# Transform tables brought as high and low parts by GpSimd's converting transfers, in a two-block sequence model on one core

## The reference, cut to what matters

```
def _hyena(hy, spec, skip):
    ...
    for o, gate in enumerate((g1, g2)):
        conv = jnp.fft.irfft(jnp.fft.rfft(z, n=2 * L, axis=1) * spec[:, o], n=2 * L, axis=1)[:, :L]
        z = gate * (conv + z * skip[o].astype(jnp.float32))
    return z
```

## Time and profile before

| what | value |
|---|---|
| median of 3 runs | 1792.31 us (1791.78 to 1796.0) |
| the profiled execution | 1793.52 us |
| its span, first to last instruction | 1791.7 us |
| mean granted TensorE clock | 0.982 |
| PE busy | 1716.9 us, 96% |
| DVE, ACT, POOL busy | 884.3, 665.2, 824.4 us |
| transferred | 167.55 MB, mean 94 GB/s |

### The profile page before, as it was taken

The page is one execution under the profiler, slowest core; times in us unless marked ns, Lnnn a source line. Parts: engine busy times, 40 slices in busy tenths (PEclk is TensorE's granted clock), DMA queues, the critical chain, the costliest instruction groups (busy, mean ns, idle before and its releaser), DMA issues.

```text
span 1791.7 us, 21383 instructions
## 1 busy us (share of the span) xinstructions
PE 1716.9 (96%) x7488; PEld 1379.8 (77%) x7488; DVE 884.3 (49%) x1172; ACT 665.2 (37%) x850; POOL 824.4 (46%) x610
## 2 busy tenths in 40 slices
PE   6899998889999999999999999999999999999996
PEld 4577776767876888888888788888888888888885
DVE  6658667774524452423256676763333432132235
ACT  4354443434422311112234657574333432222222
POOL 4225322666441454444444656555444354444443
PEclk9999999889999999999999999999999999999998
DMA  5112111224220222222222333332222232222222
GB/s 201 56 51 83 59 48 47 83 94 154 106 83 24 95 95 100 97 95 94 94 94 94 110 104 115 106 115 96 94 94 97 92 104 96 94 94 102 98 94 94
DMA packets 47343, 167.55 MB, mean 94 GB/s; under 512 B 5109, under 2 KB 5237, under 8 KB 47034
## 3 DMA queue, kind: packets, MB, share of 16 engines
q1 hardware_dynamic: 45728, 162.71, 26.1%
q10 hardware_dynamic: 1562, 4.13, 0.6%
HBM read 164.71 MB, written 2.10 MB: 93 GB/s over the span
## 4 chain that ended last, share of the span: by engine, by line
PE 43%; issue 21%; POOL 14%; DVE 2%; POOLq 0%; ACT 0%; DMA 0%; DVEq 0%; SPq 0%
POOL m_w_lo L486 14%; PE ps L525 14%; PE ps L526 14%; PE ps L527 14%; DVE m_TM L1868 0%; DVE m_h L2175 0%; DVE m_qs L1784 0%; DVE m_s L1467 0%; DVE m_ZL L1794 0%; DMA m_raw<-in_strips 0%; DVE m_s L1864 0%; POOL m_QL L504 0%; POOLq L494 0%; DVE m_QL L1856 0%; POOLq L492 0%
## 5 line engine op out<-in xcount | busy, mean ns | idle before, releaser
L486 POOL TENSOR_TENSOR m_w_lo<-m_raw,m_w_hi 128x512 fp32r<-128x512 f32 x600 | 810.1, 1373 | 930.8 <-ACT m_w_hi L1021 930.6
L1021 ACT ACTIVATE m_w_hi<-m_raw 128x1024 fp32r<-128x1024 f32 x300 | 316.6, 1057 | 627.1 <-DMA m_raw<-in_strips 626.8
L525 PE MATMUL ps<-m_XH,m_w_hi 128*128 128x512 f32 x1096 | 439.9, 401 | 4.8 <-POOL m_w_lo L486 4.5
L527 PE MATMUL ps<-m_XH,m_w_lo 128*128 128x512 f32 x1096 | 429.2, 392 | 0.0
L526 PE MATMUL ps<-m_XL,m_w_hi 128*128 128x512 f32 x1000 | 391.9, 392 | 0.0
L525 PEld LDWEIGHTS ps<-m_XH,m_w_hi 128*128 128x128 f32 x1096 | 207.5, 189 | 58.7 <-issue 9.5
L527 PEld LDWEIGHTS ps<-m_XH,m_w_lo 128*128 128x128 f32 x1096 | 207.3, 189 | 44.0
L526 PEld LDWEIGHTS ps<-m_XL,m_w_hi 128*128 128x128 f32 x1000 | 189.6, 190 | 40.5 <-issue 2.0
L525 PE MATMUL ps<-m_FH,m_w_hi 128*128 128x512 f32 x432 | 168.2, 389 | 0.3 <-DVE m_FL L1460 0.3
L526 PE MATMUL ps<-m_FL,m_w_hi 128*128 128x512 f32 x432 | 168.1, 389 | 0.0
L527 PE MATMUL ps<-m_FH,m_w_lo 128*128 128x512 f32 x432 | 168.1, 389 | 0.0
(11 more groups left out here) (344 smaller groups left out, 2243.1 us busy)
## 6 DMA issues: line engine op xcount, KB each, us to landing
m_raw<-in_strips SPq DMA_DIRECT2D x300, 512.0 KB, 3.2
m_x_in<-in_x SPq DMA_DIRECT2D x4, 512.0 KB, 11.6
m_x_res<-in_x ACTq DMA_DIRECT2D x1, 2048.0 KB, 8.5
out<-m_h SPq DMA_DIRECT2D x8, 256.0 KB, 2.1
m_decay<-in_decay ACTq DMA_DIRECT2D x1, 1024.0 KB, 10.2
m_memf<-in_mem SPq DMA_DIRECT2D x1, 1024.0 KB, 16.5
m_w<-in_w ACTq DMA_DIRECT2D x1, 512.0 KB, 8.0
m_const<-in_const ACTq DMA_DIRECT2D x1, 256.0 KB, 6.8
```

Source lines behind the costliest of these rows:

```text
L486: nc.gpsimd.tensor_tensor(w_lo[:, c], raw[:, c], f(w_hi[:, c]), ALU.subtract).then_inc(lo_ready, 1)
L525: pe.matmul(dst, w_hi[:, c], xh, start=first, stop=False)
L527: return pe.matmul(dst, w_lo[:, c], xh, start=False, stop=last)
L1021: act.activation(w_hi[:, c], raw[:, c], ACT.Copy).then_inc(hi_ready, 1)
```

## The change

The eleven table strips are split before the launch. The array of strips keeps their values rounded to the coarse format, and a new array `tables` holds the differences. For a table SP issues nothing, ScalarE computes nothing and only passes the signal on, and GpSimd issues two transfers, one into `w_hi` and one into `w_lo`. Their destination type is float32r and their source type float32, so they convert. Both signal the one semaphore `tab_in`. GpSimd waits for both before it signals `lo_ready`, ahead of everything that follows in its program. Strips up to 55 are written out one by one on SP and GpSimd, where there had been a loop.

```diff
+TABLES = tuple(range(S_SPEC, S_SPEC + N_SPEC)) + HY_STRIPS[0] + HY_STRIPS[1]
...
+            for n in range(RING, S_WOUT):
+                sp.wait_ge(pe_done, n - RING + 1)
+                if n not in TABLES:
+                    load(n, n % RING)
...
             def lows(first, end):
 
-                full, rest = divmod(end - first, RING)
-                if full:
+                for n in range(first, min(end, S_WOUT)):
+                    if n in TABLES:
+                        c = slice(n % RING * STRIP, (n % RING + 1) * STRIP)
+                        pool.wait_ge(pe_done, n - RING + 1)
+                        pool.dma_start(w_hi[:, c], A["strips"][n]).then_inc(tab_in, 16)
+                        pool.dma_start(w_lo[:, c], A["tables"][TABLES.index(n)]).then_inc(tab_in, 16)
+                    pool.wait_ge(hi_ready, n + 1)
+                    if n in TABLES:
+                        pool.wait_ge(tab_in, 32 * (TABLES.index(n) + 1))
+                        pool.wait_ge(lo_ready, 2 * n)
+                        pool.sem_inc(lo_ready, 2)
+                    else:
+                        low(n % RING)
...
-                act.wait_ge(landed[slot], count * 16)
                 c = slice(slot * STRIP, (slot + 1) * STRIP)
-                act.activation(w_hi[:, c], raw[:, c], ACT.Copy).then_inc(hi_ready, 1)
+                if n in TABLES:
+                    act.wait_ge(hi_ready, n)
+                    act.sem_inc(hi_ready, 1)
+                else:
+                    act.wait_ge(landed[slot], count * 16)
+                    act.activation(w_hi[:, c], raw[:, c], ACT.Copy).then_inc(hi_ready, 1)
...
+    tables = all_strips[list(TABLES)]
+    coarse = ((tables.view(np.uint32) + np.uint32(0x800)) & np.uint32(0xFFFFF000)).view(np.float32)
+    all_strips[list(TABLES)] = coarse
```

More of the change, by code:

```diff
@@ L299, in build @@
         hi_ready = sem("hi_ready")
+        tab_in = sem("tab_in")
         lo_ready = sem("lo_ready")
@@ L446, in load @@
             def load(n, slot):
-                sp.dma_start(raw[:, slot * STRIP:(slot + 1) * STRIP], A["strips"][n]).then_inc(landed[slot], 16)
+                c = slice(slot * STRIP, (slot + 1) * STRIP)
+                sp.dma_start(raw[:, c], A["strips"][n]).then_inc(landed[slot], 16)
             def x_pair(i):
@@ L462, in _ @@
             sp.dma_start(memf[:], A["mem"]).then_inc(ld_mem, 16)
-            full, rest = divmod(N_STRIPS - RING, RING)
+            for n in range(RING, S_WOUT):
+                sp.wait_ge(pe_done, n - RING + 1)
+                if n not in TABLES:
+                    load(n, n % RING)
+            full, rest = divmod(N_STRIPS - S_WOUT, RING)
             with sp.Fori(0, full) as i:
                 for u in range(RING):
-                    sp.wait_ge(pe_done, i * RING + u + 1)
+                    sp.wait_ge(pe_done, i * RING + (S_WOUT - RING + u + 1))
                     sp.dma_start(raw[:, u * STRIP:(u + 1) * STRIP],
-                                 A["strips"][bass.ds(i * RING + (RING + u), 1)].rearrange("a p c -> (a p) c")
+                                 A["strips"][bass.ds(i * RING + (S_WOUT + u), 1)].rearrange("a p c -> (a p) c")
                                  ).then_inc(landed[u], 16)
             for u in range(rest):
-                n = RING + full * RING + u
+                n = S_WOUT + full * RING + u
                 sp.wait_ge(pe_done, n - RING + 1)
@@ L488, in lows @@
             def lows(first, end):
-                full, rest = divmod(end - first, RING)
-                if full:
+                for n in range(first, min(end, S_WOUT)):
[11 more added lines that the diff above has]
+                        low(n % RING)
+                if end > S_WOUT:
+                    full, rest = divmod(end - S_WOUT, RING)
                     with pool.Fori(0, full) as i:
                         for u in range(RING):
[L494 to L498, removed]
+                            pool.wait_ge(hi_ready, i * RING + (S_WOUT + u + 1))
+                            low((S_WOUT + u) % RING)
+                    for n in range(end - rest, end):
+                        pool.wait_ge(hi_ready, n + 1)
+                        low(n % RING)
             def product_low(o, j):
@@ L1017, in high, with loads @@
             def high(n, slot, count):
-                act.wait_ge(landed[slot], count * 16)
                 c = slice(slot * STRIP, (slot + 1) * STRIP)
-                act.activation(w_hi[:, c], raw[:, c], ACT.Copy).then_inc(hi_ready, 1)
+                if n in TABLES:
[4 more added lines that the diff above has]
+                    act.activation(w_hi[:, c], raw[:, c], ACT.Copy).then_inc(hi_ready, 1)
+            def loads(n):
+                return n // RING + 1 - sum(t < n and t % RING == n % RING for t in TABLES)
             def ahead(n):
@@ L1026, in ahead @@
                 if m < N_STRIPS:
-                    high(m, m % RING, m // RING + 1)
+                    high(m, m % RING, loads(m))
             def ahead_in(turn, per, n):
                 m = n + 3
-                high(None, m % RING, turn * (per // RING) + (m // RING + 1))
+                high(None, m % RING, turn * (per // RING) + loads(m))
             def root(n, dst=rstd):
@@ L2315 @@
     arrays = {
-        "strips": all_strips, "const": const, "feat": features, "w3": w3,
+        "strips": all_strips, "tables": tables - coarse, "const": const, "feat": features, "w3": w3,
         "decay": decay.reshape(TT, P, T).transpose(1, 0, 2).reshape(P, TT * T),
```

## The result

The changed kernel takes 1798.88 us (median of 20 runs, 1793.47 to 1803.8), the kernel before 1792.37 us (20 runs, 1784.46 to 1797.05). The ratio is 1.0036, 95% interval [1.0023, 1.005]: slower, by 6.5 us. Measured again later it was 1799.79 against 1791.99 us, ratio 1.0046 [1.0028, 1.0063]. The forecast was 1800.7, range 1788 to 1823.

The account below looks back on a forecast made before the run. The prediction took PE as the bound, busy 1716.9 of 1791.7 us. Late values in the Hyena stage (+9.2 us) and the filter's spectrum (-0.8) gave +8.4 on 1792.3, so 1800.7 us, range 1788 to 1823.

Parts of the forecast that it names:

- The mechanism: Hyena stage: GpSimd idles about 7 us per table, seven times; PE waits 6 us and 10 us for its QL.
- X: Time from GpSimd being free to issue a table's first transfer until both halves are complete; taken as 7.0 us.
- The bound of 5.0 us for the pair: Lower bound for landing a table's two 512 KB transfers, from SP's loads: 3.2 + 1.8 us.
- The rule: Whole kernel's change in us: 7X - 40.6 above X = 5.7, 4X - 23.5 below; break-even at X = 5.8.
- the rule's tail: Hyena stage, from the end of QL(1,0) to the values: 13.8 us of work plus 0.3 for handovers, 14.1 us.
- The sign of being wrong: End of the Hyena stage: values beginning before 412 us, instead of near 419, would point to A.
- ScalarE's relief: Roundings of about 1.06 us removed from ScalarE; claimed to reach PE in one place only, -0.8 us.
- Ahead of the filter's spectrum: Rounding of strip 10 precedes the squares of `mem`, whose sum holds PE 0.82 us; removing it gives -0.8 us.
- Costed at nothing: Tables 8 to 10, table 32, the 11 extra halves (5.6 MB), SP's skipped loads and written-out loops: no cost.
- A: Rival: table transfers as quick as SP's, X = 5.0 to 6.5, change -3.5 to +4.9 us; chance 0.34.
- B: Rival: VectorE holds up GpSimd's transfer descriptors, X = 9.6, change +26.6 us, 1819 us; chance 0.12.
- C: Rival: converting halves the transfer rate, X = 10.6, change +33.6 us, 1826 us; chance 0.08.

Follow-up runs that it names:

- e1: Changed kernel, but TensorE instead of GpSimd waits for each table to land, one semaphore per slot: 1782.32 us, ratio 0.9955 against the kernel before.
- e3: Kernel before with only tables 44 to 47 handled the new way: 1795.85 us, ratio 1.0036 against the kernel before.
- e4: Kernel before with only tables 8, 9, 10 and 32 handled the new way: 1790.86 us, ratio 1.0001 against the kernel before.
- e5: Changed kernel, but GpSimd issues a table's second transfer only when its first has landed: 1813.22 us, ratio 1.0125 against the kernel before.
- e6: Changed kernel with only the first 128 of 1024 columns of each table half transferred: 1785.53 us, ratio 0.9965 against the kernel before.
- e2: Kernel before with only tables 37, 38 and 39 handled the new way: 1796.11 us, ratio 1.003 against the kernel before.
- e7: Kernel before without GpSimd's low parts of the eleven tables; TensorE's third matmul reads the high part instead: 1783.41 us, ratio 0.9947.
- e8: e1 with the 2 MB transfer of x issued some 20 us later, behind strip 54's rounding: 1785.55 us, ratio 0.9959 against the kernel before.
- e9: The changed kernel run once more, unaltered, for a second profile: 1799.79 us, ratio 1.0046 against the kernel before.

## Why the prediction was right, and where its numbers were off

**The mechanism** held: GpSimd waits inside its program, the products behind the tables come late, and PE waits for them. PE's two largest waits are those named, 7.3 us at inverse(0,1) (6 forecast) and 6.3 at inverse(1,0) (10 forecast); in the second profile 5.7 and 10.0. e1, e3 and e4 show it by taking it away and by placing it, e5 and e6 by making X longer and shorter. A table kept GpSimd for 5.1 to 7.4 us, where about 7 were forecast.

**X was mis-sized**: 7.0 forecast, 6.0 and 6.3 measured, 6.15 in the mean. At 7 us per us this term made the forecast 6 us too high. The bound of 5.0 us for the pair was met where nothing else was in transit: both halves of table 37 had landed 5.0 us after the first issue, of table 45 4.9 to 5.0. That includes the two issues (0.53 to 0.57 us each), so the 1.2 us for them were counted twice, and of the 0.8 us for VectorE (the rows that it names give 0.95) nothing is to be seen. What was left out is the meeting with SP's loads: X is 5.3 in the mean for tables 37 and 45, and 6.3 (5.1 to 7.4) for 38, 39, 46 and 47, beside which a strip is loaded. That is read from traces, no run took these loads away. Table 44, with no strip beside it, took 6.8 and 7.3; why is open.

**The rule** for the stage nearly held. With the stage's start at 315.4 it reads 54.5 + 7X above the kink and 71.6 + 4X below it, in us to the values:

| | X | rule | measured |
|---|---|---|---|
| e6 | 3.5 | 85.6 | 84.0 |
| changed, first profile | 6.0 | 96.5 | 98.4 |
| changed, second profile | 6.3 | 98.6 | 100.2 |
| e5 | 8.2 | 111.9 | 113.5 |

Three of the four are 1.6 to 1.9 us above the rule. e6's nearness is in part chance: its first inverse ended 43.4 us after the stage's start, where the rule below the kink keeps the first profile's 47.6.

**What made up for X.** By the rule alone X = 6.15 gives 97.6 - 94.2 - 0.8 = +2.5 us, and 6.5 to 7.8 were measured. Three terms make up the difference.

First, the kernel before was read in a slow execution of its stage: 94.2 us, against 90.6 in its second profile and 90.2 in e4. Of the 3.6 us between its profiles 2.4 are inverse(0,3), which took 5.3 us in the first (363.04 - 357.78) and 2.8 in the second and in e4, behind the same wait of 2.7 us: the lower clock that the prediction read from the earlier trace rows does not follow that wait each time. Behind the changed kernel's longer wait it did: inverse(0,1) to (0,3) took 10.9 us, the 5.3 + 2.8 + 2.8 of the forecast. Against the mean of both, the rule gives 1.8 us more.

Second, the rule's tail is too short: from the end of QL(1,0) to the values it has 14.1 us, and the changed kernel, e5 and e6 take 15.7. GpSimd's low of strip 48 and its two QLs take 8.1 for 7.4, and VectorE's product of step 3 ends 2.3 us behind them, for 1.3.

Third, from the values to the query projection the changed kernel takes 74.1 and 72.9 us, the kernel before 71.2 and 71.1, 2.4 in the mean. This was not foreseen, the two traces were to run in parallel from there: PE waits 2.1 and 2.5 us for strip 51 instead of 0.8. The traces point to a meeting that the late QL(1,0) brings about. In the changed kernel, e3, e5 and e6 strip 50's load is issued within some 1.5 us of the transfer of x; that transfer takes 9.9 to 12.7 us, strip 51's load 6.2 to 7.0, and PE waits 1.8 to 2.5. In the kernel before, e1, e2, e4 and e7 the load goes out 3.8 to 4.0 us ahead of x, and the same three are 8.2 to 8.5, 4.9 to 5.3 and 0.7 to 0.9 us. No run moved x in the changed kernel itself, so this is read from traces and not tested.

That the forecast lay 2 us from the result is thus partly luck: X was too high by 6 us, and what was too low makes up for 4 to 5 us by the medians (the three terms add up to 6 by the profiled executions).

**The sign of being wrong** that was named, values before 412 us, came true in the first profile (408.75) and not in the second (414.91). It was a bad sign: the stage's start alone scatters from 309.65 to 318.0 us. From its start the values come after 98.4 and 100.2 us, where the forecast has 103.5.

**ScalarE's relief** reaches PE in a second place, which the prediction denied. The rounding of strip 37 (329.46, 1.06 us) had stood on ScalarE ahead of XH, from which VectorE makes the XL that PE waits for; without it PE's wait ahead of keys(2) falls from 2.3 to 1.2 us, first before, then changed:

```profile
332.03 1.35 PE L748 MATMUL ps<-m_const,m_TM 128*128 128x128 f32 x8 [2.29 <-DVE m_XL L1822]
```

```profile
325.48 1.31 PE L768 MATMUL ps<-m_const,m_TM 128*128 128x128 f32 x8 [1.23 <-DVE m_XL L1850]
```

So it is in all twelve profiles: 1.2 us where strip 37 skips ScalarE, 2.0 to 2.4 where it does not, and the 48 matmuls of keys(2) and keys(3) behind it take 5.8 us, against 6.9 and 7.3 in the kernel before. In the changed kernel this gain is lost, since the chain that ends last runs through GpSimd.

**Ahead of the filter's spectrum**, PE's wait of 0.82 us is in both profiles before, and in no kernel where tables 8 to 10 skip ScalarE (changed, e1, e4, e5, e6, e8 and e9); in e2, e3 and e7, which keep the rounding, it is 0.8 to 1.1. The step was right, but e4's time shows nothing of it, its interval being 2.9 us to either side.

**Costed at nothing** (tables 8 to 10, 32, SP's loop): right by e4. The extra halves are 5.8 MB, not 5.6 (173.33 against 167.55 MB).

**The rivals.** A was nearer than its chance said: X = 6.0 lies inside it. What decided against it are the three terms above, not X. B is not borne out: GpSimd's 22 issues take 0.53 to 0.70 us, whatever VectorE does, and table 37 was complete after 5.0 us while VectorE was busy 4.2 of 5.1 us. The rule of the Trainium skill named there ("SBUF — State Buffer", SBUF: two separate sides) is for VectorE in a two-port mode. VectorE mostly ran two-input instructions beside the issues, and no run put another kind there, so the rule itself was not tested. C is not either: the second converted half of 512 KB lands 4.7 us after its issue in the median, and the queue of converting transfers filled 2.0% of the 16 engines' span for 11.54 MB, as SP's 26.3% for 156.94 MB.

## What to carry to other kernels

A wait moved into an engine's program costs its length for everything queued behind it, times the number of such waits in a row: count what stands behind, not what the engine saves. Here the arithmetic taken from GpSimd was worth 9 us, and the waits put in its place cost more than that; giving the wait to the consumer (e1) kept the gain, and at 1782.3 us it is, with e8 beside it within the intervals, the fastest version that computes everything. Compare stages from their own start, and take two profiles of the baseline before trusting a difference of a few us.

## What was not expected of the hardware

Eleven subtractions on GpSimd that PE did not wait for in this stage were worth 9 us. GpSimd and VectorE delay each other: an L1868 pair took 3.55 us in the first and 3.44 us in the second profile before, 2.33 and 2.34 in the changed kernel and e7, and 1.29 in e1. The chain ends in ZL, for which PE waits; in e7 forward(1,0) follows keys(4) after 12.4 us in place of 16.4, and forward(1), no longer behind a wait of over 4 us, takes 11.2 in place of 12.8 and 13.5. That is about 6 of the 9 us; the rest was not traced.

Four converting pairs issued nearly together (e1, tables 44 to 47) took 6.9 and 8.3 us in the median from issue to landing, against 3.8 and 4.7 one pair at a time. PE's wait of 2.7 us there is not shown to come from that: it is for the low part of table 44, the first of the four, which landed 6.2 us after its issue, and 5.7 and 6.2 us after it in the changed kernel, where its pair was alone.
